# Query projection of a latent-attention layer: from whole float32 products, head by head, to three float32r products of high and low parts, two heads at a time

## The reference, cut to what matters

```python
def mla_project(h, pos, w_in, q_norm, kv_norm, w_qb, w_uk):
    z = h @ w_in
    q_a, c, kr = jnp.split(z, [Q_LORA, Q_LORA + KV_LORA], axis=-1)
    q = (rmsnorm(q_a, q_norm) @ w_qb).reshape(B, T, MLA_HEADS, NOPE_DIM + ROPE_DIM)
    q_nope, q_rope = q[..., :NOPE_DIM], q[..., NOPE_DIM:]
    q_lat = jnp.einsum('bthn,rhn->bhtr', q_nope, w_uk)
    q_rope = rope(q_rope, pos).transpose(0, 2, 1, 3)
```

## Time and profile before

| | |
|---|---|
| device time of the profiled execution | 2231.13 us |
| its span from first to last instruction | 2229.5 us |
| three runs | 2231.09, 2235.38, 2235.84 us |
| PE busy over the whole span | 2012.7 us (90%) |
| the q block in the span | about 121.3 to 205.8 us |

### The profile page before, as it was taken

How to read it: one execution, slowest core, us unless ns; L and a number is a source line. 1 busy time by engine, 2 the same in 40 slices (tenths; PEclk the granted TensorE clock), 3 DMA queues, 4 the chain that set the end, 5 groups by cost and what they waited for, 6 DMA issues and landing times. The chain is left out here.

```text
span 2229.5 us, 51187 instructions
## 1 busy us (share of the span) xinstructions
PE 2012.7 (90%) x22040; PEld 1797.7 (81%) x22040; DVE 904.8 (41%) x1491; ACT 641.8 (29%) x1057; POOL 126.1 (6%) x167
## 2 busy tenths in 40 slices
PE   4789889998899999995799889999998899999995
PEld 3656557776899999994699759988944899999995
DVE  5323541223253433335943164445253353333334
ACT  2112434443142212222533333333120232212222
POOL 0001000340000000000000020000131000000000
PEclk7889999998999999997899989999885999999998
DMA  4012401783223232321222100001030222232321
GB/s 125 20 51 71 138 0 44 244 245 117 59 77 92 76 95 85 89 72 27 59 82 76 29 2 4 4 4 41 4 102 19 67 76 85 77 100 79 89 72 40
DMA packets 229240, 158.06 MB, mean 71 GB/s; under 512 B 12504, under 2 KB 221247, under 8 KB 228928
## 3 DMA queue, kind: packets, MB, share of 16 engines
q1 hardware_dynamic: 223412, 136.93, 20.8%
q0 software_dynamic: 5376, 18.36, 2.7%
q10 hardware_dynamic: 268, 0.08, 0.0%
HBM read 149.96 MB, written 5.34 MB: 70 GB/s over the span
## 5 line engine op out<-in xcount | busy, mean ns | idle before, releaser
L311 PE MATMUL ps<-ffn_xh,ffn_wh 128*128 128x280 f32 x1408 | 299.0, 294 | 18.0 <-DVE ffn_xl L1360 13.7
L311 PE MATMUL ps<-ffn_xh,ffn_wl 128*128 128x280 f32 x1408 | 297.2, 292 | 0.0
L311 PE MATMUL ps<-ffn_xl,ffn_wh 128*128 128x280 f32 x1408 | 296.3, 292 | 0.0
L311 PEld LDWEIGHTS ps<-ffn_xh,ffn_wh 128*128 128x128 f32 x1408 | 225.8, 190 | 19.0 <-issue 18.8
L311 PEld LDWEIGHTS ps<-ffn_xh,ffn_wl 128*128 128x128 f32 x1408 | 225.6, 190 | 0.0
L311 PEld LDWEIGHTS ps<-ffn_xl,ffn_wh 128*128 128x128 f32 x1408 | 224.6, 190 | 0.0
L1262 ACT CAST ffn_wh<-wa 128x1024 fp32r<-128x1024 f32 x88 | 91.3, 1041 | 208.0 <-PE ps L311 180.4
L311 PE MATMUL ps<-ffn_hid_h,ffn_wh 128*128 128x280 f32 x704 | 148.0, 291 | 0.0
L311 PE MATMUL ps<-ffn_hid_h,ffn_wl 128*128 128x280 f32 x704 | 147.6, 291 | 0.0
L311 PE MATMUL ps<-ffn_hid_l,ffn_wh 128*128 128x280 f32 x704 | 147.5, 291 | 0.0
L317 DVE TENSOR_TENSOR ffn_wl<-wa,ffn_wh 128x1024 fp32r<-128x1024 f32 x88 | 107.7, 1225 | 87.2 <-ACT ffn_wh L1262 87.2
(11 more groups left out here) (355 smaller groups left out, 3625.5 us busy)
## 6 DMA issues: line engine op xcount, KB each, us to landing
wa<-in_ffn_w_gate SPq DMA_DIRECT2D x44, 512.0 KB, 3.7
wa<-in_ffn_w_up SPq DMA_DIRECT2D x44, 512.0 KB, 3.7
arena<-in_cache SPq DMA_DIRECT2D x77, 160.0 KB, 3.4
wb<-in_ffn_w_down SPq DMA_DIRECT2D x16, 768.0 KB, 4.6
wb<-in_ffn_w_down SPq DMA_DIRECT2D x16, 640.0 KB, 4.3
arena<-in_cache POOLq DMA_DIRECT2D x63, 160.0 KB, 3.5
wb<-in_cache SPq DMA_DIRECT2D x40, 160.0 KB, 3.5
wb<-in_cache POOLq DMA_DIRECT2D x28, 160.0 KB, 3.6
```

The source lines that it names most:

```text
L311: mm = nc.tensor.matmul(dst[:, s, 0:HALF], a[:, c * width:(c + 1) * width], b[:, c, s * HALF:(s + 1) * HALF], start=first and n == 0, stop ...
```

## The change

The q block now goes over four pairs of heads, written out instead of in a hardware loop.

- Every product is three float32r products of high and low parts. The high parts of q_a (`q_xh`), of the weights (`wqh`, two buffers, one pair each), of the nope result (`qnh`) and of the transposed `w_uk` (`ukh`) are copies of ScalarE; the low parts are subtractions of VectorE.
- The weights of a pair are cut (`cut_w`) one pair ahead: ScalarE and VectorE cut pair i + 1 before they turn to the results of pair i. A slot of `w_qb` is given back by VectorE's cut, no longer by TensorE.
- The rope columns of two heads lie side by side and make one tile of 128 columns; VectorE turns it with seven operations a pair (`rope_pair`). The constants `cos` and `sin` are laid out for 128 partitions.
- TensorE does a pair as: nope of the even head, nope of the odd head, rope of both, four transposes of `w_uk`, then the four latent products.
- SyncE's loads keep their order. The four credits are gone.

The core of the diff:

```diff
@@ sync
-                with sp.Fori(1, H // 2) as i:
+                for i in range(1, PAIRS):
                     for u in range(2):
-                        wa.load(sp, u, wa.view(u, QC, NOPE + ROPE), w_qb[:, :, i * 2 + u], i)
+                        wa.load(sp, u, raw_q(u), w_qb[:, :, i * 2 + u], i)
                         wa.load(sp, 2 + u, wa.view(2 + u, RC, P), w_uk[:, :, i * 2 + u], i)
@@ tensor
+                for i in range(PAIRS):
                     for u in range(2):
+                        pe.wait_ge(wa.used[u], of_turns(i, u))
+                        ge(pe, lat_kept, 4 * (i - 1) + 3 + u)
+                        project(i, 2 * u, slice(u * NOPE, (u + 1) * NOPE)).then_inc(q_nope, 1)
+                    ge(pe, rope_read, i)
+                    project(i, 4, slice(2 * NOPE, WQ)).then_inc(q_rope, 1)
+                    ge(pe, uk_low, i)
+                    for u in range(2):
                         wa.wait_full(pe, 2 + u, i)
                         for c in range(RC):
-                            mm = nc.tensor.transpose(ps[:, 4, c * P:(c + 1) * P], wu[:, c], ident)
+                            mm = nc.tensor.transpose(ps[:, 6, u * KL + c * P:u * KL + (c + 1) * P], wa.view(2 + u, RC, P)[:, c], ident)
                         mm.then_inc(wa.used[2 + u], 1)
+                    pe.wait_ge(uk_low, i + 1)
+                    for u in range(2):
+                        for c in range(RC):
+                            if u == 0:
+                                pe.wait_ge(nope_low, 2 * i + c + 1)
+                            else:
+                                pe.wait_ge(lat_kept, 4 * i + c + 1)
+                            at = slice(u * KL + c * P, u * KL + (c + 1) * P)
+                            product(2 * c, ukh[:, at], ukl[:, at], qnh[:, u], qnl[:, u], True, True).then_inc(lat_done, 1)
@@ scalar
+                cut_w(0, 0)
+                for c in range(QC):
+                    nc.scalar.copy(q_xh[:, c], hT[:, c]).then_inc(x_high, 1)
+                cut_w(0, 1)
+                for i in range(PAIRS):
+                    if i + 1 < PAIRS:
+                        for u in range(2):
+                            cut_w(i + 1, u)
...
+                    nc.scalar.copy(ukh[:, :], ps[:, 6, 0:2 * KL]).then_inc(uk_high, 1)
@@ vector
+                def cut_w(i, u):
+                    dve.wait_ge(w_high, 2 * i + u + 1)
+                    for dst, src in places(u):
+                        low = take_low(wql[:, i % 2, :, dst], raw_q(u)[:, :, src], wqh[:, i % 2, :, dst])
+                    low.then_inc(wa.used[u], 1)
...
+                    if i + 1 < PAIRS:
+                        for u in range(2):
+                            cut_w(i + 1, u)
+                    for u in range(2):
+                        dve.wait_ge(nope_high, 2 * i + u + 1)
+                        take_low(split(qnl[:, u]), halves(2 * u), split(qnh[:, u])).then_inc(nope_low, 1)
+                    dve.wait_ge(uk_high, i + 1)
+                    take_low(ukl[:, :], ps[:, 6, 0:2 * KL], ukh[:, :]).then_inc(uk_low, 1)
+                    rope_pair(i)
```

More of the change, by code:

```diff
@@ L116, in constants @@
     ang = (inv[:, None] * pos[None, :]).astype(np.float32)
-    put("cos", np.concatenate([np.cos(ang), np.cos(ang)]))
-    put("sin", np.concatenate([-np.sin(ang), np.sin(ang)]))
+    put("cos", np.concatenate([np.cos(ang)] * 4))
+    put("sin", np.concatenate([-np.sin(ang), np.sin(ang)] * 2))
     put("window", np.arange(4 * DC - 2)[None, :] == 2 * (DC - 1) + p[:, None] // RH, later)
@@ L444, in program @@
         z, at = carve(at, ZC, T)
-        qn, at = carve(at, 2, T)
-        ukT, at = carve(at, 2, KL)
         rt, at = carve(at, 2, T)
+        q_room = at
         norm = Norm("mix0", xT, hT, "ln_mix0", DC)
@@ L557, in _, with raw_q, places, of_turns @@
                 sp.wait_ge(keys_out, 16 * 12)
-        q_nope, q_lat0, q_lat1, nope_kept = (sem(n) for n in ("q_nope", "q_lat0", "q_lat1", "nope_kept"))
-        uk_kept, lat0_kept, lat1_kept, roped = (credit(n) for n in ("uk_kept", "lat0_kept", "lat1_kept", "roped"))
+        WQ = 2 * (NOPE + ROPE)
+        q_xh, q_xl = as_r("q_xh", "arena", after_keys, QC, T), as_r("q_xl", "hT", QC * T, QC, T)
+        ukh, ukl = as_r("q_ukh", "arena", after_keys + QC * T, 2 * KL), as_r("q_ukl", "arena", after_keys + QC * T + 2 * KL, 2 * KL)
+        assert QC * T + 4 * KL <= ZC * T
+        qnh, qnl = as_r("q_nh", "arena", q_room, 2, T), as_r("q_nl", "arena", q_room + 2 * T, 2, T)
+        wqh, wql = as_r("q_wh", "arena", q_room + 4 * T, 2, QC, WQ), as_r("q_wl", "arena", q_room + 4 * T + 2 * QC * WQ, 2, QC, WQ)
+        assert q_room + 4 * T + 4 * QC * WQ <= ARENA
+        x_high, x_low, w_high, q_nope, q_rope, nope_high, nope_low, uk_high, uk_low, lat_done, lat_kept, roping, rope_read, roped = (
+            sem(f"q_{n}") for n in ("x_high", "x_low", "w_high", "nope", "rope", "nope_high", "nope_low", "uk_high", "uk_low",
+                                    "lat", "lat_kept", "roping", "rope_read", "roped"))
+        PAIRS = H // 2
+        def raw_q(u):
+            return wa.view(u, QC, NOPE + ROPE)
+        def places(u):
+            return ((slice(u * NOPE, (u + 1) * NOPE), slice(0, NOPE)),
+                    (slice(2 * NOPE + u * ROPE, 2 * NOPE + (u + 1) * ROPE), slice(NOPE, NOPE + ROPE)))
+        def of_turns(n, u):
+            return n + wa.base[u] + 1 + FREE
         with nc.Block(no_gpsimd_drain=True) as block:
@@ L571, in _, with product @@
             def _(pe):
-                with pe.Fori(0, H // 2) as i:
-                    for u in range(2):
[L574 to L582, removed]
+                def product(bank, wh, wl, xh, xl, first, last):
+                    for n, (a, b) in enumerate(((wh, xh), (wh, xl), (wl, xh))):
+                        for s in range(2):
+                            mm = nc.tensor.matmul(ps[:, bank + s, 0:HALF], a, b[:, s * HALF:(s + 1) * HALF],
+                                                  start=first and n == 0, stop=last and n == 2)
+                    return mm
@@ new lines, in project @@
+                def project(i, bank, cols):
+                    for c in range(QC):
+                        if i == 0:
+                            pe.wait_ge(x_low, c + 1)
+                        mm = product(bank, wqh[:, i % 2, c, cols], wql[:, i % 2, c, cols], q_xh[:, c], q_xl[:, c], c == 0, c == QC - 1)
+                    return mm
+                for i in range(PAIRS):
+                    for u in range(2):
+                        pe.wait_ge(wa.used[u], of_turns(i, u))
[5 more added lines that the diff above has]
+                    for u in range(2):
@@ L583, in _ @@
                         wa.wait_full(pe, 2 + u, i)
-                        pe.wait_ge(uk_kept, h + FREE)
                         for c in range(RC):
-                            mm = nc.tensor.transpose(ps[:, 4, c * P:(c + 1) * P], wu[:, c], ident)
+                            mm = nc.tensor.transpose(ps[:, 6, u * KL + c * P:u * KL + (c + 1) * P], wa.view(2 + u, RC, P)[:, c], ident)
                         mm.then_inc(wa.used[2 + u], 1)
-                        pe.wait_ge(roped, h * 4 + FREE)
@@ L603, in _ @@
             @block.scalar
             def _(act):
-                with act.Fori(0, H // 2) as i:
-                    for u in range(2):
[L607 to L615, removed]
+                def cut_w(i, u):
+                    wa.wait_full(act, u, i)
+                    ge(act, q_rope, i - 1)
+                    for dst, src in places(u):
+                        cp = nc.scalar.copy(wqh[:, i % 2, :, dst], raw_q(u)[:, :, src])
+                    cp.then_inc(w_high, 1)
@@ new lines, in _ @@
+                cut_w(0, 0)
+                for c in range(QC):
+                    nc.scalar.copy(q_xh[:, c], hT[:, c]).then_inc(x_high, 1)
[4 more added lines that the diff above has]
+                            cut_w(i + 1, u)
+                    for u in range(2):
+                        act.wait_ge(q_nope, 2 * i + u + 1)
+                        nc.scalar.copy(split(qnh[:, u]), halves(2 * u)).then_inc(nope_high, 1)
+                    for u in range(2):
+                        act.wait_ge(wa.used[2 + u], of_turns(i, 2 + u))
+                    nc.scalar.copy(ukh[:, :], ps[:, 6, 0:2 * KL]).then_inc(uk_high, 1)
+                    for u in range(2):
+                        for c in range(RC):
+                            act.wait_ge(lat_done, 4 * i + 2 * u + c + 1)
+                            nc.scalar.copy(split(q[:, c, 2 * i + u]), halves(2 * c)).then_inc(lat_kept, 1)
@@ L617, in _, with cut_w @@
             @block.vector
             def _(dve):
-                with dve.Fori(0, H // 2) as i:
-                    for u in range(2):
-                        h = i * 2 + u
-                        dve.wait_ge(wa.used[u], i + (wa.base[u] + 1) + FREE)
-                        rope(2, split(q[0:ROPE, 2, h]), roped, h * 4 + FREE)
+                def cut_w(i, u):
```

(31 more changed lines are left out.)

## The result

The changed kernel takes 2239.99 us (median of 11 runs, 2237.86 to 2243.09) against 2231.42 us (11 runs, 2227.26 to 2235.84): a ratio of 1.0038 with a 95% interval of 1.0028 to 1.0047. It is 8.6 us slower; 9.5 had been forecast.

What follows compares the result with a forecast made beforehand. PE was taken to bound the q block. Shorter PE work, against three gaps of 8.8 us and half-clock latent products, summed to 94.1 us against 84.55, 9.5 more: 2240.6 or 2244.9 by base, 2243 stated, range 2234 to 2250.

Steps and rivals of the forecast that it cites:

- the sum of 9.5 us: q block: first pair, three turns and last pair's end give 94.1 us against 84.55, so 9.5 us more.
- PE's work: q block: 96 float32r matmuls a pair plus four transposes (0.95 us), 13.3 us against 20.3 for two heads before.
- Four pairs would save 28 us if PE never waited: q block: saving from PE's shorter work alone, 13.3 us a pair against 20.3, without any waits.
- The gap: Between a pair's transposes and latent products PE idles 8.8 us, three times, for the odd head's w_qb load, cuts and subtractions.
- the bounds: Allowances on load, latent products, ACT's and DVE's chain, w_qb's runs and first pair: together +5.5 to +13 us.
- The estimate of 2.9 us: w_qb load of 384 KB: about 2.0 us plus bytes at 436 GB/s; the forecast used the rows' 3.6 and 4.3.
- The clock: Falls 3.6 us into each gap; 24 latent matmuls then take 4.7 to 5.3 us, not 3.1; 5.0 taken.
- the rival that it holds: Clock stays up in the gaps: latent products take 3.1 us, total +3.8 us, about the same time; chance 0.09.
- The block: q block: first pair's transposes end at 14.7 us, three turns of 24.05, end at 94.1 against 84.55 us.
- The other blocks: Blocks outside the q block have the same instructions; no time was added for them.
- The rival on the faster side: Odd w_qb load early enough: turn 15.0 us, 17.6 us less, 2217.8 us; chance 0.06.
- the signs of being wrong: Gaps under 6 us, first two transposes not releasing the load, or another block changing length.

Runs made afterwards that it cites:

- e1: Changed kernel with SyncE issuing both w_qb loads of a pair ahead of both w_uk loads: 2217.62 us, ratio 0.9935 to the kernel before.
- e2: Changed kernel with ACT and DVE cutting the next pair's odd head at the end of a turn, loads unmoved: 2215.72 us, ratio 0.9932 to the kernel before.
- e5: e4 with one whole float32 matmul in place of each three float32r products, low parts computed but unread: 2216.67 us, ratio 0.9936 to the kernel before.
- e4: Changed kernel with PE doing a pair's four transposes ahead of its nope products, SyncE's order kept: 2206.66 us, ratio 0.9888 to the kernel before.
- e3: Changed kernel with eight idle float32 products on PE behind the transposes of the first three pairs: 2234.33 us, ratio 1.0012 to the kernel before.
- e9: Kernel before with the q block's loops over pairs written out on all four engines: 2227.72 us, ratio 0.9998 to the kernel before.
- e10: e9 without GpSimd's four credits ahead of the q block: 2231.61 us, ratio 1.0009 to the kernel before.

## Why the prediction was right

Inside the block the mechanism held in each step, and e1 and e2 show it from both sides: PE waits for a load that its own transposes release, because ACT and DVE stand in line behind that load. The forecast of 2243 us and the direction came out. That the sum of 9.5 us lies so near the measured 8.6 is partly luck, since two errors cancel: the block grew 2.9 us less than the sum says, and by the medians 2.0 us (8.6 less 6.6) lie outside it, where nothing had been put.

- *PE's work.* Three products at 0.386 us against 0.455 was right: e5, with whole products in e4's order, is 10 us slower, and 9 had been expected. Behind the first gap of the changed kernel 72 projection matmuls took 9.35 us (148.23 to 157.58), 0.390 for three; whole ones took 0.47 in e5. The four transposes took 0.60 us (134.23 to 134.83), where 0.95 was read. "Four pairs would save 28 us if PE never waited": e4 shows 26 us in the block's stretch (86.8 to 60.8).
- *The gap* was sized at 8.8 us and is 8.0, 7.8 on average of three (25.0 less the last 1.5). The load took 3.8 us from issue to first use where I took 4.1 with the median of four in a row. DVE's five subtractions took 2.9 (139.88 to 142.80), not 3.3: they follow each other faster than their durations add up, which was kept in the bounds and not in the sum. The estimate of 2.9 us from the Trainium skill (DMA: Bandwidth & Descriptors, "Anatomy of one DMA — SWDGE (gpsimd) path") was too short by 0.9; that path is GpSimd's, and this load is SyncE's.
- *The clock* fell in each gap, and the rival that it holds is out. The latent products took 5.4 to 5.8 us, above the 4.7 to 5.3 that was allowed: the clock came back 4.4, 5.1 and 6.0 us after their start, not 3.6 to 4.9, and at a clock of 1.00 they take 3.6 us (e3), not 3.1. Both terms were some half a microsecond too low, so their difference held: e3 prices the clock at 5.7 us in all, and three times 1.9 had been worked out.
- *The block* grew by 6.6 us, not 9.5: a turn of 23.3 instead of 24.05, and a first pair of about 14 instead of 14.7. This is the part of the sum that was too large: the shorter gap and transposes outweigh the longer latent products.
- *The other blocks.* "The other blocks have the same instructions" was true, and the conclusion that they take the same time was not: the recurrent stage took 4 to 5 us more in the two pairs of profiles, more than the 2.0 by the medians; the stretch behind it wanders by more than 3 us between executions. That term stood at zero. The prediction had named it among the signs of being wrong ("or if another block changes length"): on this point it was wrong, and the cause is open.
- *The rival on the faster side* named the right lever: with the load early, e1 has a turn of 15.0 us, as worked out, and a stretch some 18 us shorter where 17.6 was. That e1's 2217.62 meets the 2217.8 is luck: the rival started from 2235.38, and e1's gain is 13.4 us from 2231.05.

## What to carry to other kernels

Where a split is moved one step ahead, ask of each load in the queue what must happen before it is issued, and what stands behind its first reader: a load that waits for late work of the engine it feeds closes a ring, and in-order queues let the ring hold up results that have nothing to do with it. Here the ring could be opened in three places: the release early (e4, some 33 us better than the change), the loads in another order (e1, 22), or the reader last (e2, 24). An idle gap on TensorE is priced with the slow matmuls behind it. And blocks with the same instructions need not take the same time: read them in both traces before the whole difference is put down to the block that was changed.

## What had not been expected

- The clock fell 2.2 us into the first gap (0.52 in the window at 137, idle since 134.83), 2.8 us into the second (0.97 at 160, idle since 158.2) and 3.4 us into the third (0.91 at 184, idle since 181.4), each time sooner than the 3.6 us of the earlier trace rows; where PE is kept busy with products nobody reads (e3) it stays at 1.00.
- A stage a thousand us later takes 2 to 10 us more with every variant of the new block, and neither spare semaphores, written-out loops nor credits reproduce it.
- Dropping the credits gains nothing: the stretch from the last write to the next block's first load is 86.2 us in e9 and 86.4 in e10, though 0.4 us of PE's wait had been put down to them.
